# Expert rows gated as they leave PSUM, one more round through DRAM, and round 0's down product moved ahead in a mixture-of-experts stage

## What is computed

```
mod = silu(cond) @ w_mod + b_mod              # g2 is one sixth of it: one row for context, one for latent
x   = x + g1 * token_mixer(...)
h   = modulate(rms_norm(x), sh2, sc2)
for e in range(16):
    hid = silu(h @ exp_gate[e]) * (h @ exp_up[e])          # 1024 -> 512
    out = out + combine[:, e:e+1] * (hid @ exp_down[e])    # 512 -> 1024
y = x + g2 * out                                           # g2 differs between context and latent rows
```

## Time and profile before

| what | value |
|---|---|
| time, median of 3 runs | 908.45 us (908.08 to 908.51) |
| the profiled execution's own time | 910.12 us |
| its span in the trace | 908.2 us |
| TensorE busy | 844.1 us (93%) |
| VectorE busy | 434.3 us (48%) |
| ScalarE busy | 251.6 us (28%) |
| mixture-of-experts rounds | from about 602 us to the end |

### The profile page before, as it was taken

One profiled execution on the slowest core, in us unless ns is written; L12 is line 12 of the kernel. 1 busy time (PEld: TensorE's weight loads), 2 busy tenths in 40 slices (PEclk: granted clock), 3 DMA queues, 4 the chain that ended last, 5 costly groups with the idle time before them and its releaser, 6 DMA issues. The chain is left out here.

```text
span 908.2 us, 18989 instructions
## 1 busy us (share of the span) xinstructions
PE 844.1 (93%) x8238; PEld 481.1 (53%) x8238; DVE 434.3 (48%) x895; ACT 251.6 (28%) x492; POOL 88.9 (10%) x136
## 2 busy tenths in 40 slices
PE   5999999999989995799998799997999999999997
PEld 3555555545556774688888555442344443334333
DVE  4321366222557885768887568654231000002258
ACT  5002222322678772223322302222111111111110
POOL 1180000000000000222221000210000000000040
PEclk9999999999999996799999899998999999999999
DMA  9999999673890000002222494288999999999693
GB/s 342 332 254 408 374 396 352 233 265 113 308 390 32 14 12 29 12 5 61 85 63 58 109 317 189 115 307 339 422 411 427 426 426 428 427 427 426 244 340 117
DMA packets 72548, 227.90 MB, mean 251 GB/s; under 512 B 10644, under 2 KB 15820, under 8 KB 66064
## 3 DMA queue, kind: packets, MB, share of 16 engines
q1 hardware_dynamic: 61120, 201.38, 58.4%
q0 software_dynamic: 5552, 16.95, 5.2%
q10 hardware_dynamic: 5792, 8.35, 2.4%
HBM read 166.98 MB, written 59.67 MB: 250 GB/s over the span
## 5 line engine op out<-in xcount | busy, mean ns | idle before, releaser
L2471 PE MATMUL ps<-arena 128*32 128x512 f32 (+2 forms) x832 | 170.6, 609 | 6.0 <-DMA arena<-in_exp_gate_dram 5.5
L2471 PEld LDWEIGHTS ps<-arena 128*32 128x32 f32 (+2 forms) x832 | 59.4, 135 | 106.7 <-issue 106.1
L1015 PE MATMUL ps<-arena 128*128 128x128 f32 (+1 forms) x384 | 106.8, 435 | 0.0
L1015 PEld LDWEIGHTS ps<-arena 128*128 128x128 f32 x384 | 58.4, 190 | 50.6 <-issue 48.9
L2338 PE MATMUL ps<-arena 128*128 128x512 f32 x160 | 72.1, 596 | 2.0 <-PEq L1519 2.0
L2523 PE MATMUL ps<-arena 128*32 128x512 f32 (+2 forms) x368 | 70.7, 594 | 0.0
L751 DVE SCALAR_TENSOR_TENSOR arena<-arena 128x128 f32<-128x128 f32 (+3 forms) x56 | 30.9, 552 | 69.9 <-ACT arena L658 68.4
L894 PE MATMUL ps<-arena 128*128 128x512 f32 (+1 forms) x160 | 52.4, 486 | 0.0
L2971 DVE TENSOR_TENSOR arena<-arena,ps 128x512 f32<-128x512 f32 x12 | 8.2, 687 | 89.3 <-ACT arena L2231 89.3
L2338 PEld LDWEIGHTS ps<-arena 128*128 128x128 f32 x160 | 29.1, 190 | 33.6 <-issue 33.6
L2523 PEld LDWEIGHTS ps<-arena 128*32 128x32 f32 (+2 forms) x368 | 23.7, 130 | 39.4 <-issue 38.6
(11 more groups left out here) (412 smaller groups left out, 1330.3 us busy)
## 6 DMA issues: line engine op xcount, KB each, us to landing
gathered_tokens<-arena SPq DMA_DIRECT2D x16, 2560.0 KB, 21.1
arena<-in_exp_up_dram SPq DMA_DIRECT2D x16, 2048.0 KB, 18.4
arena<-in_exp_gate_dram SPq DMA_DIRECT2D x16, 2048.0 KB, 16.0
arena<-in_exp_down_dram SPq DMA_DIRECT2D x16, 2048.0 KB, 17.2
arena<-in_w_mod_dram SPq DMA_DIRECT2D x12, 2048.0 KB, 15.0
arena<-in_w_in_dram SPq DMA_DIRECT2D x4, 2048.0 KB, 12.7
expert_outputs<-arena ACTq DMA_DIRECT2D x10, 512.0 KB, 10.6
arena<-in_x_sample_dram SPq DMA_DIRECT2D x8, 512.0 KB, 9.3
```

Source lines behind the costliest of these rows:

```text
L1015: mm = pe.matmul(ps[:, b, 0:hi - lo], ring_of(what)[:, k, (e % 4) * P:(e % 4) * P + P], hT[:, k, lo:hi], start=(k == 0), stop=(k == KT - 1))
L2471: mm = pe.matmul(ps[c:c + m, b, :], xgT[:, k, c:c + m], w[n % 3][:, k, :], start=(k == 0), stop=(k == KT - 1))
```

## The change

Four things are changed together.

- **Gate at the exit from PSUM.** `prompt_slots` works out which slots hold context rows, `slot_gates(r)` builds the g2 row of each slot in the place where the output will lie, and `y_out(r)` multiplies PSUM by it, both halves on VectorE. `early_sum` has two passes in place of three, `final` one in place of up to two, and the `gated` halves and ScalarE's copies of results are gone.
- **Round 10 through DRAM.** `STORED` is 11. Only round 11 stays on the chip, so `late_rows` has one matmul where it had two, and the gathers wait for the store of round 10.
- **Round 10's down product ahead of the last gate product.** `down(9)` and `down(10)` both stand ahead of `gate_up(11)`; round 10 uses PSUM banks and buffers of its own.
- **Round 0's down product sooner.** `down(0)` stands ahead of `x_turn(1)` and `gate_up(1)`; it stood behind `gate_up(1)` and `x_turn(2)`. SyncE's order of loads is as before.

The core of the diff:

```diff
-STORED = sum(CAPQ) // 4 - 2
+STORED = sum(CAPQ) // 4 - 1
...
+        def y_rows(r):
+            return xg[1] if r == STORED - 1 else y_last if r == STORED else yo
+        def hid_turned(r):
+            return hidT_next if r == STORED - 1 else hidT
+        def down_bank(r):
+            return XT0 if r == STORED - 1 else Y0
...
                 def down(r):
                     weights_landed(r, "down")
                     pe.wait_ge(hT6_ok, r + 1)
-                    if r:
-                        pe.wait_ge(yo_a, r)
-                        pe.wait_ge(yo_v, r)
+                    if r == STORED - 1:
+                        pe.wait_ge(xgT_ok, NR)
+                    elif r:
+                        pe.wait_ge(yo_ok, min(r, STORED - 1))
...
-                x_turn(1)
                 h_turn(0)
                 pe.wait_ge(slot_ok, 3)
-                for r in range(1, NR):
+                down(0)
+                x_turn(1)
+                for r in range(1, STORED):
                     gate_up(r)
-                    if r + 1 < NR:
-                        x_turn(r + 1)
-                    if r <= STORED:
+                    x_turn(r + 1)
+                    if r == STORED - 1:
+                        pe.wait_ge(hT6_ok, r)
+                        h_turn(r)
+                    if r > 1:
                         down(r - 1)
+                    if r < STORED - 1:
                         h_turn(r)
...
+                down(STORED - 1)
+                gate_up(STORED)
+                h_turn(STORED)
+                down(STORED)
...
                 def early_sum(tt):
                     dve.wait_ge(got[tt], 32)
                     ch(dve.scalar_tensor_tensor(yA[tt], yB[tt], e2[:, tt:tt + 1], yA[tt], ALU.mult, ALU.add))
-                    ch(dve.scalar_tensor_tensor(yA[tt], yA[tt], wsel[:, 0, tt:tt + 1], gate2[:, 1 if tt else 0], ALU.mult, ALU.mult))
-                    ch(dve.tensor_tensor(yA[tt], yA[tt], xs2[:, tt, :], ALU.add))
+                    ch(dve.scalar_tensor_tensor(yA[tt], yA[tt], wsel[:, 0, tt:tt + 1], xs2[:, tt, :], ALU.mult, ALU.add))
...
+                def slot_gates(r):
...
+                    ch(dve.tensor_scalar(y_rows(r), gate2[:, 0], of_prompt[:, 0, r:r + 1], None, ALU.mult))
+                    ch(dve.scalar_tensor_tensor(y_rows(r), gate2[:, 1], of_prompt[:, 1, r:r + 1], y_rows(r), ALU.mult, ALU.add))
+                def y_half(r, half):
+                    cols = slice(512 * half, 512 * half + 512)
+                    return dve.tensor_tensor(y_rows(r)[:, cols], y_rows(r)[:, cols], ps[:, down_bank(r) + half, :], ALU.mult)
...
                 hidden(0)
+                prompt_slots()
                 hot = overflow_table()
-                for r in range(1, NR):
+                overflow_rows(hot)
+                dve.wait_ge(ld_g2b, 32)
+                slot_gates(0)
+                y_out(0)
+                for r in range(1, STORED):
                     hidden(r)
...
+                slot_gates(STORED - 1)
+                y_out(STORED - 1)
+                gated_hidden(STORED)
+                slot_gates(STORED)
+                up_hidden(STORED)
                 early_sum(1)
                 early_sum(2)
-                gated(0, 0)
-                gated(0, 1)
-                gated(1, 0)
+                dve.wait_ge(y6_mm, NR)
+                y_half(STORED, 0).then_inc(yo_ok, 1)
                 early_sum(3)
-                gated(1, 1)
+                dve.wait_ge(y6_mm, NR + 1)
+                y_half(STORED, 1).then_inc(yo_ok, 1)
                 early_sum(0)
```

More of the change, by code:

```diff
@@ L2134, in _ @@
                 with sp.If(more > 0):
-                    sp.wait_ge(late_mm, 4)
+                    sp.wait_ge(y6_mm, NR + 1)
                     sp.wait_ge(st7, 32 * NTT)
@@ L2238, in oh_out, with y_store @@
                     act.wait_ge(oh_mm, b + 1)
[L2239 to L2245, removed]
+                    if b:
+                        act.activation(slot_a, ps[:, 7, 0:P], ACT.Copy).then_inc(oh_ok, 1)
+                    else:
+                        act.activation(slot_b, ps[:, 7, :].rearrange("p (c t) -> p c t", t=P), ACT.Copy).then_inc(oh_ok, 1)
                 def h_out(r):
                     act.wait_ge(hT6_mm, r + 1)
-                    act.activation(hidT if r < NR - 1 else hidT_last, ps[:, HT, :].rearrange("p (k t) -> p k t", t=P), ACT.Copy).then_inc(hT6_ok, 1)
-                def y_out(r):
-                    act.wait_ge(y6_mm, r + 1)
-                    if r:
[L2254 to L2258, removed]
+                    act.activation(hid_turned(r), ps[:, HT, :].rearrange("p (k t) -> p k t", t=P), ACT.Copy).then_inc(hT6_ok, 1)
+                def y_store(r):
+                    act.wait_ge(yo_ok, r + 1)
+                    act.dma_start(yg_d[r * P:(r + 1) * P, :], y_rows(r)).then_inc(y_st, 16)
                 sum_squares(0)
@@ L2923, in result_rows @@
                     dve.tensor_copy(back_i[:, :], limit_f.rearrange("p r t -> p (r t)")).then_inc(early_ok, 1)
-                    for i in range(3):
+                    for i in range(2):
                         ch(dve.tensor_scalar(rel[:, i], back_f, -float((STORED + i) * P), None, ALU.add))
@@ L2945, in weights_by_row @@
                     for a, n in enumerate(BATCHES7[b]):
-                        ch(weight_of(ch, by_row[a], n // NTT, n % NTT))
+                        ch(weight_of(ch, by_row[a], 0, n))
                     dve.tensor_copy(one_choice[:, 0:1], by_row[0][:, 0:1]).then_inc(m7_ok, 1)
-                def gated(i, half):
-                    cols = slice(512 * half, 512 * half + 512)
-                    dve.wait_ge(yc_ok, 2 * i + half + 1)
-                    dve.tensor_tensor(y_gated[i][:, cols], y_plain[i][:, cols], gate2[:, 1, cols], ALU.mult).then_inc(yl_ok, 1)
                 def early_sum(tt):
```

144 lines of the change are left out of this document (68 added, 76 removed).

## The result

The changed kernel took 919.86 us (median of 4 runs, 916.9 to 921.27), the kernel before 908.48 (908.08 to 908.8): ratio 1.0121, 95% interval 1.0096 to 1.0146. It is slower by 11.4 us. The prediction said slower, by 6.1: 914.5, with a range to 919.5. The median lies 0.4 above that range; the ratio applied to the 908.45 that the prediction started from gives 919.4, at its very end. The profiled execution has a span of 919.5 us against 908.2.

The account below looks back on a forecast made before the run. The prediction took TensorE to bound the rounds, and store, gathers and VectorE the last 60 us. +12.1 at the start and -6.0 in the tail gave +6.1, so 914.5 us, with a range from 910.5 to 919.5.

Parts of the forecast that it names:

- The start: Start of the rounds on TensorE: down(0) waits for its down weights and delays all later rounds, +12.1 us.
- the 0.6 of the gather: Start of the rounds: the gather of round 3's rows now waits for x_turn(1), which takes back 0.6 us.
- The clock's cost: Start of the rounds: TensorE's longer wait brings a lower granted clock, 3.0 us; bounds nothing and twice that.
- T: The end of gate_up(10), from which the forecast counts the tail; 847.39 in the kernel before.
- the rounds' new work: Rounds: VectorE's slot_gates and second output half lie beside down(r - 1) and cost nothing; uncovered, 3.3 us a round.
- the fast rival: Start of the rounds: down(0)'s weights land early enough, the hole is filled, and the time is 905.5; 9%.
- The tail: From the end of gate_up(10) to the span's end: T + 54.8 in place of T + 60.8, -6.0 us.
- the queues are empty at about T + 22.4, and so I take 5.2 us for this store: Tail: round 10's store, issued at T + 17.2, takes 5.2 us; gathered rows are there at T + 29.9.
- the gap after round 11's join: Tail: a VectorE gap there would show the forecast wrong, as the sign of the late store.
- 3.7 us from VectorE's end to the span's: End of the program: VectorE ends at T + 51.1, the span at T + 54.8.
- some 3: Tail: estimated us for a store alone, 1.2 of transfer and the rest of a gather's 5.45.
- the store comes late too: Tail: round 10's store takes 11.4 us, gathered rows come at T + 36.1, and the time is 920; 13%.

Follow-up runs that it names:

- e1: Changed kernel with round 0's down product and rows back behind round 1's products; ratio 0.998 to the kernel before.
- e2: Changed kernel with round 0's late down weight loaded first of its group of four instead of third; ratio 0.9998 to the kernel before.
- e6: Changed kernel without the down-weight loads of the last two experts, so its output is not the layer's; ratio 1.0074 to the kernel before.
- e5: Kernel before with only the gates in the expert rows of rounds 0 to 9 and sums of two passes; ratio 0.9968 to the kernel before.
- e12: Changed kernel without its part on round 10, with round 0's second down weight loaded early; ratio 0.9981 to the kernel before.
- e3: Changed kernel with round 0's late down weight loaded some 20 us earlier, ahead of the last pair of scatters; ratio 0.9953 to the kernel before.
- e9: Changed kernel with round 0's down product back in place and the last down-weight load held until round 10's store landed; ratio 0.995 to the kernel before.
- e4: Kernel before with only the load of round 0's second down weight moved early; ratio 1.0055 to the kernel before.
- e11: Changed kernel with round 0's second down weight loaded early and the last down-weight load held until round 10's store landed; ratio 0.9959 to the kernel before.

## Why the prediction was right or wrong

**The start** was right in mechanism and nearly in size. The wait: 16.97 us, forecast about 17. The load's landing: 17.2 after issue, forecast 17.6. `down(0)` started at 638.84 (638.16), round 1's products at 650.85 (about 650.5), round 2's at 666.99 (666.0, the 666.6 less the 0.6 of the gather). The clock's cost: `down(0)` took 9.80 in place of 7.09, 2.7 us, at a granted clock of 0.50 to 644 us, where the forecast took 3.0. T came 13.2 us later, forecast 12.1; 0.4 of the difference is P0's. e1 shows that this one move carries all of the loss, and that the rounds' new work is hidden as claimed.

That the load is late was put down to its place, third in the queue. e2 shows it: first in the same queue, issued at the same point, it took 8.06. The rule of the Trainium skill ("DMA: Bandwidth & Descriptors", section on the anatomy of one DMA) that gave the fast rival is a fit for single DMAs that GpSimd issues. This load is one of four that SyncE issues together: 6.8 us by the rule, measured 17.2 in third and 8.06 in first place.

**The tail** is the step that failed: -6.0 forecast, -1.9 measured. The step "the queues are empty at about T + 22.4, and so I take 5.2 us for this store" put 5.2 where 8.15 was measured, and with the gathers behind it VectorE started at T + 33.1, not at T + 30.5: 2.6 us, the gap after round 11's join that the prediction had named as the sign of a late store. Its work took 20.87, not 20.6: 0.3. And the term that I carried over without thought, 3.7 us from VectorE's end to the span's, was 4.9: 1.2. With the 1.1 at the start (T at 860.60, forecast 859.5) these 4.1 us are the 5.2 between the forecast span, 914.3, and 919.5.

The sum was otherwise sound: in e6, where the store lies alone, VectorE starts at T + 30.4, works 20.7 and the tail is 55.8, beside the forecast 54.8. So the forecast tail needs a store that nothing shares, which the program doesn't give. My count of bytes had the two loads and two stores end at T + 22.4 (its terms, 8.6 + 10 + 2.5 + 1, give 22.1); the two loads, issued at T + 8.9 and T + 10.0, landed after 9.0 and 14.8 us, the second at T + 24.8, and the store at T + 25.4.

Two smaller terms of the tail were off as well. The lower bound of "some 3" for a store alone doesn't follow from the row that it names either, since 1.2 and the rest of 5.45 make 5.45; e6 then measured 2.6. And `down(11)`, put at 7.0, took 8.78, with a granted clock of 0.62 from 892.5 to 897 us, and ended at T + 41.0 in place of T + 38.9; VectorE used its second half only at 902.65, so this cost nothing.

The rival "the store comes late too" gave the right time, 920, for half the right reason: the store lay between its 11.4 and my 5.2, and the rest was at the two ends. 13% was too little for it, and the range should have taken in a store of 8 together with a dearer clock.

The end of the span, the 4.9 us, is ten stores of 256 KB that SyncE issues (line 2133), the last ones at VectorE's pace of 0.6 us each. The view of that line (ns of one issue min/median/max, first and last start):

```profile
L2133 SPq DMA_DIRECT2D out_dram<-arena x10: 332/332/1444, 906.6 to 915.5; - x10
...
DMA to landing us min/median/max: 2.0/2.5/3.6
```

One issue, the last but one, took 1.44 us from 914.03 on, where the median is 0.33. So the last store was issued at 915.5, 0.9 us after VectorE's last pass; in the kernel before, the longest issue took 0.42, the last store was issued at 904.5, as VectorE ended, and the slowest landed after 3.3 us. Of the 1.2 us, 0.9 is thus a late issue and 0.3 a slower landing. The stores crowd there, by stretch (length, busy of PE, PEld, DVE, ACT and POOL, granted clock, DMA share, GB/s):

```profile
911.00:914.00 3.00, 1.45 (x4) 0.38 (x2) 3.00 (x7) 0.00 (x0) 0.00 (x0) 1.00 0.95 346
914.00:917.00 3.00, 0.00 (x0) 0.00 (x0) 0.59 (x1) 0.00 (x0) 0.00 (x0) 1.00 0.83 307
```

256 KB each 0.6 us is 437 GB/s, more than the 346 that they got. All profiled runs with round 10 through DRAM end 4.6 to 4.9 us after VectorE, e5 and e12, where VectorE's last passes follow TensorE's late rows, 2.4. In e3 the last store was issued on time, but its slowest landed after 4.4, and the end was as late. That the crowding is the reason, of the late issue too, is argued from these numbers and was not tried alone.

## What to carry to other kernels

A hole on the bounding engine can only be filled with work whose operands are there: read the landing of each operand, not its place in the list, before you move an instruction ahead of it. A load that is pulled forward isn't free either; look for the small transfers that share its engines and ask who waits for them, here a scatter that gates four loads. At the end of a program, a chain store, gather, sum is longer by what the traffic beside its store costs (8.15 us for a store of 2.6), and an engine that finishes sooner can hand its gain to the next one in line (the late rows of TensorE in e5, the gathers in e9, the output stores here).

## What the runs showed of the hardware

First, the indirect scatter is the fragile transfer. With 4 MB of weights ahead of it in another queue it took 3.6 to 4.3 us in ten profiled runs; with 6 MB, 8.9 to 9.8 (e3, e4, e11, e12). In the changed kernel the last of the weights landed 1.3 us after this scatter's issue, in e3 7.7 us after it. The 512 KB store took 2.6 us alone, 7.7 to 8.3 beside two weight loads and 10.6 beside full queues. The Trainium skill says in "DMA: Bandwidth & Descriptors" (section on queues, rings and completion order) that each DMA engine goes round the queues it has work for, one packet at a time. The changed kernel's trace agrees with it: round 9's store, issued at 870.73, landed after 11.3 us, at 882.0, ahead of a weight load that was issued at 870.58 and landed at 885.4. What a turn costs no run here shows, and in e3 the scatter landed 1.9 us after the last of the three weight loads, so for it the traces don't tell taking turns from waiting for their end.

The second thing: a pass of VectorE with one tensor operand and a per-row scalar over 128x1024 f32 took 0.75 us, where the one with two tensor operands takes 1.28. I had taken 1.3 for both; "VectorE: DVE Perf Modes" in the Trainium skill states a factor of two for such a pass with one source in SBUF, and the trace agrees in direction, with 1.7 between the two passes. It changed nothing here, since that work is hidden. VectorE's timeline in e6:

```profile
879.40 0.75 DVE L2983 TENSOR_SCALAR arena<-arena 128x1024 f32<-128x1024 f32 x1
880.18 1.28 DVE L2984 SCALAR_TENSOR_TENSOR arena<-arena 128x1024 f32<-128x1024 f32 x1
```
